# Joint key products, a second key bank, and the spatial gate's statistics, norm and scaling on other engines

## Chip, cores and metric

One core of one Trainium2 chip runs the kernel. The metric is the device time of one execution in microseconds (us), as the median of several runs.

## What is computed

The kernel is a two-layer encoder on 512 positions of width 1024. The change touches the first mixer of each layer, which is two head groups side by side: attention over a low-rank cache (8 heads, keys of 64 + 32 columns), and a spatial gate. Cut to that part:

```python
for l in range(DEPTH):                                   # 2 layers
    h = rmsnorm(x, norm_mix_g[l]); proj = h @ w_in[l]
    # A: attention, 8 heads
    q  = rmsnorm(h_q) @ w_uq;  q_nope, q_pe = split, rope
    kv = rmsnorm(h_kv) @ w_ukv;  k_nope, v = split       # (512, 8, 64) each
    s  = q_nope @ k_nope.T + q_pe @ k_pe.T
    o_mla = softmax(s * scale) @ v
    # B: spatial gate
    u, v = split(gelu(h_sg))                             # 512 columns each
    v = layernorm(v, ln_g, ln_b)
    o_sg = u * (W_s @ v + b)                             # per head, in chunks of 128 positions
    x = x + concat(rmsnorm(o_mla), rmsnorm(o_sg)) @ w_out
    ...                                                  # memory attention, gated MLP
```

## The kernel before

**Numbers in halves.** Every factor of a product is split into a rounded part and a remainder (`_hi`, `_lo`), and each product is three matmuls (`product3`, L1387 to L1389): hi by hi, hi by lo, lo by hi. Weights come in blocks through `raw`; ScalarE rounds a block (`split`, L459), GpSimd takes the remainder (`low`, L358), and TensorE uses both. There are four slots, and `ahead(b)` rounds block b + 3.

**Steps.** Attention runs over 8 heads h and 4 blocks t of 128 queries. A step is the pair (h, t), with i = 4h + t. Each engine has its own program with this loop written out by hand, and tables such as `STAT_STEPS` say in which step an extra piece stands. Engines wait for each other only by counting semaphores (`need`), and each engine keeps strictly to its own order. In step i:

- TensorE: `scores(i+4)` (three matmuls into one of banks 5, 6, 7, once `exps(i+1)` is done), `turn(i)` (four transposes of the exponentials into bank i % 2, L1543, once `exps(i)` and `turned_lo(i-2)` are done); at t = 0 `spread_sums(h-1)` (L1571); at t = 1 and 2 half of `attend(h-1)` each; at t = 3 `q_proj(h+3)`, and at t = 1 `k_proj(h+2)`.
- ScalarE: `exps(i+3)` (L606, with a sum over the row), `turned_hi(i)` (L614), and at fixed steps `q_part` (L593), `k_part` (L600), `copy_sums` (L622), a block to round (L459) and pieces of the gate.
- VectorE: `amax(i+4)` (L1085), `turned_lo(i)` (L1111), and at fixed steps `q_part` (L1062), `k_part` (L1067), `attended` (L1097), `recip_sums` and pieces of the gate.
- GpSimd: `low` for the blocks, and the remainders of queries (`query_low`, L371) and of the gate's normed input (`gate_low`, L376).

**Banks of the keys.** Each head's key product fills 64 of 128 rows, and from head 2 on it shares bank 4 with the query product:

```python
def q_bank(h):
    return (4, 6)[h] if h < 2 else 4

def k_bank(h):
    return (5, 7)[h] if h < 2 else 4
```

So `k_proj(h)` waits until VectorE has read the query (`qf_done`), and `q_proj(h+1)` until VectorE has read the key (`kl_done`).

**The gate.** ScalarE's GELU writes `vt` (L655). VectorE takes its mean and variance (`statistics`, L1115 and L1117), ScalarE and VectorE make the inverse root (`small_root`), VectorE normalises (L1170, L1172, two operations a chunk), ScalarE rounds (L695), GpSimd takes the remainder. TensorE mixes in four parts (`mix`, bank 2), VectorE gates `u` (L1127), ScalarE squares it (L684) and later scales it (L688), and TensorE turns it (`turn_gated`, L1600) in head 7.

## Time and profile before

| | us |
|---|---|
| median of 3 runs (lowest, highest) | 1498.18 (1496.62, 1498.19) |
| profiled execution: its time | 1497.97 |
| profiled execution: its span | 1496.2 |
| TensorE busy | 1460.7 |
| VectorE busy | 748.4 |
| ScalarE busy | 692.1 |
| GpSimd busy | 646.5 |

Matmuls overlap in the array, so TensorE's busy time counts the overlap as well, and it is not the number of matmuls times their pitch. What a stage loses is seen from the starts of its matmuls and from the idle time that the timeline prints before a row, with the instruction that ended it.

### The profile page before, as it was taken

What the parts mean: (1) busy time and instruction counts of PE and PEld (TensorE: products, weight loads), DVE (VectorE), ACT (ScalarE), POOL (GpSimd) and SP (SyncE); (2) the same over time, 40 slices, a digit from 0 to 9 for tenths busy, and PEclk for the clock granted to TensorE, in tenths of its full rate; (3) what the DMA queues carried; (4) which work ended last, traced back from release to release, by engine and by line L of the source; (5) the groups of instructions that cost most, each with busy time, mean ns of one, the idle gap of its engine ahead of it and who ended that gap; (6) DMA issues with size and microseconds to landing.
All of it is one profiled execution on the core that took longest, in us unless ns stands there. A gap on an engine that the chain in (4) does not pass through costs nothing.

```text
span 1496.2 us, 19445 instructions
## 1 busy us (share of the span) xinstructions
PE 1460.7 (98%) x6876; PEld 1196.7 (80%) x6876; DVE 748.4 (50%) x1154; ACT 692.1 (46%) x1107; POOL 646.5 (43%) x313
## 2 busy tenths in 40 slices
PE   8999999999999999999999999999999999999996
PEld 7776689888888888888878776888888888888884
DVE  7648578343355420445264776781526544024534
ACT  6566746354354421344355775553534444124432
POOL 2433148644343554354445322684343454435350
PEclk9999999999999999999999999999999999999998
DMA  5320225412233333232323102453031332323231
GB/s 204 101 82 15 70 82 158 143 56 71 61 106 101 112 99 99 85 104 80 121 80 98 55 29 71 127 183 99 29 99 57 113 112 81 116 85 100 77 91 57
DMA packets 38888, 138.75 MB, mean 93 GB/s; under 512 B 4448, under 2 KB 4704, under 8 KB 38560
## 3 DMA queue, kind: packets, MB, share of 16 engines
q1 hardware_dynamic: 37872, 134.25, 29.3%
q10 hardware_dynamic: 944, 3.51, 0.7%
q8 instruction: 49, 0.80, 0.2%
q14 instruction: 23, 0.19, 0.0%
HBM read 135.64 MB, written 2.10 MB: 92 GB/s over the span
## 4 chain that ended last, share of the span: by engine, by line
PE 74%; issue 10%; DVE 8%; ACT 4%; POOL 4%; DMA 0%; SPq 0%; POOLq 0%; DVEq 0%; ACTq 0%
PE ps L1387 24%; PE ps L1388 24%; PE ps L1389 24%; POOL w_lo L358 4%; DVE small L1085 1%; ACT work L606 1%; DVE h_lo L1111 1%; DVE arena L1111 1%; DVE work L1170 0%; PE ps L1543 0%; DMA raw<-blocks_d 0%; DVE arena L1067 0%; ACT arena L614 0%; DVE work L1062 0%; DVE work L1097 0%
## 5 line engine op out<-in xcount | busy, mean ns | idle before, releaser
L358 POOL TENSOR_TENSOR w_lo<-raw,w_hi 128x1024 fp32r<-128x1024 f32 x244 | 594.5, 2454 | 704.4 <-ACT w_hi L459 704.4
L1387 PE MATMUL ps<-h_hi,w_hi 128*128 128x512 f32 (+1 forms) x1040 | 406.0, 390 | 3.5 <-DVE w_lo L900 1.7
L459 ACT ACTIVATE w_hi<-raw 128x1024 fp32r<-128x1024 f32 x247 | 255.0, 1054 | 330.8 <-PE ps L1389 327.8
L1389 PE MATMUL ps<-h_hi,w_lo 128*128 128x512 f32 (+1 forms) x1040 | 403.1, 388 | 0.0
L1388 PE MATMUL ps<-h_lo,w_hi 128*128 128x512 f32 (+1 forms) x1040 | 403.1, 388 | 0.0
L1387 PE MATMUL ps<-arena,w_hi 128*128 128x512 f32 (+2 forms) x656 | 244.3, 372 | 4.4 <-DVE work L1062 2.4
L1389 PE MATMUL ps<-arena,w_lo 128*128 128x512 f32 (+2 forms) x656 | 241.9, 369 | 0.0
L1388 PE MATMUL ps<-arena,w_hi 128*128 128x512 f32 (+2 forms) x656 | 241.8, 369 | 0.0
L1387 PEld LDWEIGHTS ps<-h_hi,w_hi 128*128 128x128 f32 x1040 | 195.2, 188 | 47.3 <-issue 3.1
L1388 PEld LDWEIGHTS ps<-h_lo,w_hi 128*128 128x128 f32 x1040 | 195.3, 188 | 40.6 <-issue 1.0
L1389 PEld LDWEIGHTS ps<-h_hi,w_lo 128*128 128x128 f32 x1040 | 195.2, 188 | 40.1
L1286 DVE TENSOR_TENSOR work<-ps,work 128x512 f32<-128x512 f32 x88 | 54.7, 684 | 216.6 <-PE ps L1389 215.7
L1387 PEld LDWEIGHTS ps<-arena,w_hi 128*128 128x128 f32 (+1 forms) x656 | 122.8, 187 | 29.3 <-DVE work L1062 5.4
L1200 DVE TENSOR_TENSOR x<-x,ps 128x512 f32<-128x512 f32 x60 | 37.5, 683 | 205.7 <-PE ps L1389 205.7
L1389 PEld LDWEIGHTS ps<-arena,w_lo 128*128 128x128 f32 (+1 forms) x656 | 122.8, 187 | 21.8
L1388 PEld LDWEIGHTS ps<-arena,w_hi 128*128 128x128 f32 (+1 forms) x656 | 122.9, 187 | 20.0
L815 ACT ACTIVATE work<-work,par 128x512 f32<-128x512 f32 x88 | 64.8, 806 | 111.2 <-DVE work L1286 111.2
L1297 DVE SCALAR_TENSOR_TENSOR work<-work,par 128x511 f32<-128x511 f32 x88 | 66.1, 752 | 12.0 <-DVE work L1294 3.1
L1294 DVE SCALAR_TENSOR_TENSOR work<-work,par 128x511 f32<-128x511 f32 x88 | 68.6, 780 | 0.0
L1085 DVE TENSOR_REDUCE small<-ps 128x1 f32<-128x512 f32 x64 | 43.5, 680 | 35.9 <-PE ps L1389 35.4
L1387 PE MATMUL ps<-arena 128*128 128x512 f32 (+2 forms) x160 | 59.9, 374 | 0.0
L821 ACT ACTIVATE work<-work 128x512 f32<-128x512 f32 x44 | 27.9, 633 | 60.5 <-DVE work L1297 60.3
(185 smaller groups left out, 1780.7 us busy)
## 6 DMA issues: line engine op xcount, KB each, us to landing
raw<-blocks_d SPq DMA_DIRECT2D x247, 512.0 KB, 3.5
work<-memT_d ACTq DMA_DIRECT2D x2, 1024.0 KB, 4.9
outT_d<-work SPq DMA_DIRECT2D x8, 256.0 KB, 2.2
x<-xT_d SPq DMA_DIRECT2D x3, 512.0 KB, 7.5
work<-ln_d ACTq DMA_DIRECT2D x2, 512.0 KB, 3.6
x<-xT_d SPq DMA_DIRECT2D x2, 256.0 KB, 4.5
raw<-blocks_d SPq DMA_DIRECT2D x2, 256.0 KB, 4.9
par<-par_d ACTq DMA_DIRECT2D x2, 113.5 KB, 3.9
```

The source lines that it names most:

```text
L358: gp.tensor_tensor(w_lo[:, b % SPLIT, :], raw[:, b % RAW, :], w_hi[:, b % SPLIT, :].bitcast(F32), ALU.subtract).then_inc(lo_done.sem, 1)
L459: act.activation(w_hi[:, b % SPLIT, :], raw[:, r, :], ACT.Copy).then_inc(hi_done.sem, 1)
L815: act.activation(conv[:, bank + 2 * j + s, :], lin[:, 2 * j + s, :], ACT.Identity, bias=cb, scale=cw).then_inc(tap1.sem, 1)
L1085: dve.tensor_reduce(low_score[:, i % 4:i % 4 + 1], ps[BS[i % 3]][:, :], AXX, ALU.min)\
L1111: dve.tensor_tensor(pt_lo[h % 2][:, :, c], ps[i % 2][:, :].rearrange("p (k q) -> p k q", k=TT), pt_hi[h % 2][:, :, c].bitcast(F32), ALU.su ...
L1200: dve.tensor_tensor(x[:, t0 + j, :], x[:, t0 + j, :], ps[banks[j]][:, :], ALU.add)\
L1286: dve.tensor_tensor(lin[:, 2 * j + s, :], ps[bank + 2 * s + j][:, :], rs, ALU.mult)\
L1294: dve.scalar_tensor_tensor(out=c[:, 1:SEQ], in0=a[:, 0:SEQ - 1], scalar=col(C_W0 + at), in1=c[:, 1:SEQ], op0=ALU.mult, op1=ALU.add).then_i ...
L1297: dve.scalar_tensor_tensor(out=c[:, 0:SEQ - 1], in0=a[:, 1:SEQ], scalar=col(C_W2 + at), in1=c[:, 0:SEQ - 1], op0=ALU.mult, op1=ALU.add).th ...
L1387: pe.matmul(out, a_hi, b_hi, start=first, stop=False)
L1388: pe.matmul(out, a_hi, b_lo, start=False, stop=False)
L1389: return pe.matmul(out, a_lo, b_hi, start=False, stop=last)
```

## The change

1. **Keys.** The keys of heads 2p and 2p + 1 come from one product of 128 rows (`k_proj(p)`): four in a layer, not eight, at steps (0, 1), (2, 1) and (4, 1) after the first. It goes to bank 5 for the first pair and to bank 2 after it, apart from the query in bank 4. The even head's half is split as before. The odd head's half sits in rows 64 to 127, so ScalarE copies it to `k_odd`, rounds it from there (`k_second`), and GpSimd takes its remainder (`key_low`).
2. **Statistics.** The GELU of `vt` also sums its rows. VectorE makes the mean in step (0, 0), and ScalarE squares the four chunks around it, with a sum, in steps (0, 1), (0, 2), (0, 2), (0, 3).
3. **Norm.** VectorE subtracts and scales in one operation a chunk, in steps (1, 0) to (1, 3); GpSimd multiplies by the gain and adds the offset, two operations a chunk (`gate_norm`). ScalarE rounds the result in (2, 0) to (2, 3).
4. **Later gating.** The third and fourth `mix` move to (4, 3) and (5, 1), the last one into bank 4. Squares and root follow later, and the scaling of `u` moves from ScalarE to VectorE, in steps (6, 2) and (6, 3).
5. `copy_sums` stands ahead of `turned_hi` in its step, the spread of the sums fills 64 rows, and two weight blocks change places.

```diff
-STAT_STEPS = ((0, 1), (0, 2), (0, 3), (1, 0))
-ROOT_STEP = (1, 1)
-NORM_STEPS = ((1, 2), (1, 3), (2, 2), (2, 3))
-SPLIT_STEPS = ((1, 3), (2, 0), (2, 3), (3, 0))
+STAT_STEPS = ((0, 1), (0, 2), (0, 2), (0, 3))
+ROOT_STEP = (1, 0)
+NORM_STEPS = ((1, 0), (1, 1), (1, 2), (1, 3))
+SPLIT_STEPS = ((2, 0), (2, 1), (2, 2), (2, 3))
-MIX_STEPS = ((3, 2), (3, 3), (4, 2), (4, 3))
+MIX_STEPS = ((3, 2), (3, 3), (4, 3), (5, 1))
...
-        def k_bank(h):
-            return (5, 7)[h] if h < 2 else 4
+        def k_bank(p):
+            return 5 if p == 0 else 2
...
+                def key_low(p):
+                    need(kh_done, 2 * p + 2)
+                    gp.tensor_tensor(k_lo[0:64, 1, :], k_odd[:, :], k_hi[0:64, 1, :].bitcast(F32), ALU.subtract)\
+                        .then_inc(kodd_done.sem, 1)
+                def gate_norm(t):
+                    need(vs_done, t + 1)
+                    gp.tensor_tensor(vt[:, t, :], vt[:, t, :], ln_gb[:, 0, :], ALU.mult).then_inc(vg_mul.sem, 1)
+                    need(vg_mul, t + 1)
+                    gp.tensor_tensor(vt[:, t, :], vt[:, t, :], ln_gb[:, 1, :], ALU.add).then_inc(vn_done.sem, 1)
...
+                def k_even(p):
+                    block_used(B_HEAD[p])
+                    act.activation(k_hi[0:64, 0, :], ps[k_bank(p)][0:64, :], ACT.Copy).then_inc(kh_done.sem, 1)
+                    if p > 0:
+                        need(kodd_done, p)
+                    act.activation(k_odd[:, :], ps[k_bank(p)][64:128, :], ACT.Copy).then_inc(kst_done.sem, 1)
+                def k_second(p):
+                    need(kst_done, p + 1)
+                    act.activation(k_hi[0:64, 1, :], k_odd[:, :], ACT.Copy).then_inc(kh_done.sem, 1)
...
+                    for c in range(TT):
+                        if (h, t) == STAT_STEPS[c]:
+                            need(vmean, 1)
+                            act.activation(sv_hi[:, c, :], vt[:, c, :], ACT.Square, bias=nmean[:, c:c + 1],
+                                           accum_out=vsq[:, c:c + 1]).then_inc(vsq_done.sem, 1)
...
-                    for c in SCALED_STEPS.get((h, t), ()):
-                        need(gated_root, 1)
-                        act.activation(u[:, c, :], u[:, c, :], ACT.Copy, scale=sm_t[:, c:c + 1])\
-                            .then_inc(sg_normed.sem, 1)
...
+                        dve.tensor_scalar(vt[:, g, :], vt[:, g, :], nmean[:, g:g + 1], sm_t[:, g:g + 1], ALU.add, ALU.mult)\
+                            .then_inc(vs_done.sem, 1)
...
+                    for c in SCALED_STEPS.get((h, t), ()):
+                        dve.tensor_scalar(u[:, c, :], u[:, c, :], sm_t[:, c:c + 1], None, ALU.mult).then_inc(sg_normed.sem, 1)
...
                     if h >= 2:
-                        need(kl_done, h)
+                        need(qf_done, h)
...
+                    c = slice(4 * P, 4 * P + 2 * NOPE)
+                    if p > 1:
+                        need(rsum_done, 2 * p - 2)
...
+                    product3(ps[k_bank(p)][:, :], wh[:, 0, c], wl[:, 0, c], ckv_hi[:, 0, :], ckv_lo[:, 0, :],
+                             True, True).then_inc(used.sem, 1)
```

TensorE, step (1, 1), before: one turn, half of `attend(0)` (the 64x512 products from `arena`), then `k_proj(3)` with its wait for the query, then the next scores.

```order
L1543 MATMUL ps<-ident,work 128x128 [waits ptl_done,exp_done]
L1543 MATMUL ps<-ident,work 128x128 x3
L1387 MATMUL ps<-arena 64x512 [waits ptl_done]
L1388 MATMUL ps<-arena 64x512
L1389 MATMUL ps<-arena 64x512
L1387 MATMUL ps<-arena 64x512
L1388 MATMUL ps<-arena 64x512
L1389 MATMUL ps<-arena 64x512
L1387 MATMUL ps<-arena,w_hi 64x512 [waits qf_done]
L1388 MATMUL ps<-arena,w_hi 64x512
L1389 MATMUL ps<-arena,w_lo 64x512
L1387 MATMUL ps<-arena 128x512 [waits exp_done]
```

The same step after the change:

```order
L1579 MATMUL ps<-ident,work 128x128 [waits ptl_done,exp_done]
L1579 MATMUL ps<-ident,work 128x128 x3
L1421 MATMUL ps<-arena 64x512 [waits ptl_done]
L1422 MATMUL ps<-arena 64x512
L1423 MATMUL ps<-arena 64x512
L1421 MATMUL ps<-arena 64x512
L1422 MATMUL ps<-arena 64x512
L1423 MATMUL ps<-arena 64x512
L1421 MATMUL ps<-arena 128x512 [waits exp_done]
L1422 MATMUL ps<-arena 128x512
```

The three key products and their wait are gone from this step; this also holds for steps (3, 1) and (5, 1).

ScalarE, from head 0's first `turned_hi` (to `arena`, waits `turned`) on, before. The rows on `work,small` are exponentials:

```order
L614 ACTIVATE arena<-ps 128x4x128 [waits turned]
L459 ACTIVATE w_hi<-raw 128x1024 [waits used,raw_in1]
L593 ACTIVATE arena<-work 128x512 [waits qf_done]
L606 ACTIVATE work,small<-ps,small 128x512 [waits turned,nmax_done]
L614 ACTIVATE arena<-ps 128x4x128 [waits turned]
L600 ACTIVATE arena<-ps 64x512 [waits kp_mm]
L606 ACTIVATE work,small<-ps,small 128x512 [waits turned,nmax_done]
L614 ACTIVATE arena<-ps 128x4x128 [waits turned]
L606 ACTIVATE work,small<-ps,small 128x512 [waits turned,nmax_done]
L614 ACTIVATE arena<-ps 128x4x128 [waits turned]
```

The same stretch after the change, from the second exponential on; L721 is the square with a sum, L632 the copy to `k_odd`:

```order
L642 ACTIVATE work,small<-ps,small 128x512 [waits turned,nmax_done]
L650 ACTIVATE arena<-ps 128x4x128 [waits turned]
L629 ACTIVATE arena<-ps 64x512 [waits used]
L632 ACTIVATE k_odd<-ps 64x512 [waits kodd_done]
L721 ACTIVATE h_hi,small<-work,small 128x512 [waits vmean]
L642 ACTIVATE work,small<-ps,small 128x512 [waits turned,nmax_done]
L650 ACTIVATE arena<-ps 128x4x128 [waits turned]
L721 ACTIVATE h_hi,small<-work,small 128x512 [waits vmean] x2
L642 ACTIVATE work,small<-ps,small 128x512 [waits turned,nmax_done]
L650 ACTIVATE arena<-ps 128x4x128 [waits turned]
L721 ACTIVATE h_hi,small<-work,small 128x512 [waits vmean]
```

Four squares and one more copy now stand among head 0's exponentials.

GpSimd in heads 0 to 2, before (L371 is `query_low`, L376 `gate_low`, L358 `low`):

```order
L371 TENSOR_TENSOR arena<-work,arena 128x512 [waits qh_done]
L358 TENSOR_TENSOR w_lo<-raw,w_hi 128x1024 [waits hi_done]
L371 TENSOR_TENSOR arena<-work,arena 128x512 [waits qh_done]
L376 TENSOR_TENSOR h_lo<-work,h_hi 128x512 [waits svh_done]
L371 TENSOR_TENSOR arena<-work,arena 128x512 [waits qh_done]
L376 TENSOR_TENSOR h_lo<-work,h_hi 128x512 [waits svh_done] x3
```

And after (L379 `query_low`, L384 `key_low`, L389 and L391 `gate_norm`, L395 `gate_low`, L366 `low`):

```order
L379 TENSOR_TENSOR arena<-work,arena 128x512 [waits qh_done]
L366 TENSOR_TENSOR w_lo<-raw,w_hi 128x1024 [waits hi_done]
L379 TENSOR_TENSOR arena<-work,arena 128x512 [waits qh_done]
L384 TENSOR_TENSOR arena<-k_odd,arena 64x512 [waits kh_done]
L389 TENSOR_TENSOR work<-work 128x512 [waits vs_done,ln_in]
L391 TENSOR_TENSOR work<-work 128x512 [waits vg_mul]
L389 TENSOR_TENSOR work<-work 128x512 [waits vs_done]
L391 TENSOR_TENSOR work<-work 128x512 [waits vg_mul]
L379 TENSOR_TENSOR arena<-work,arena 128x512 [waits qh_done]
L389 TENSOR_TENSOR work<-work 128x512 [waits vs_done]
L391 TENSOR_TENSOR work<-work 128x512 [waits vg_mul]
L395 TENSOR_TENSOR h_lo<-work,h_hi 128x512 [waits svh_done]
```

Eight operations of the norm now stand between queries and gate remainders, and the third chunk's stands behind head 4's query.

## Rows read from the trace of the kernel before

Times are in us; "L" numbers are lines of the kernel before. The two layers run the same code.

**Rows 1.** The page, its first part: busy time of each engine over the span.

```profile
PE 1460.7 (98%) x6876; PEld 1196.7 (80%) x6876; DVE 748.4 (50%) x1154; ACT 692.1 (46%) x1107; POOL 646.5 (43%) x313
```

**Rows 2.** Windows: interval, length, busy PE, PEld, DVE, ACT, POOL (instructions), granted clock.

```profile
94.71:104.05 9.34, 8.40 (x45) 6.48 (x44) 6.98 (x14) 7.59 (x16) 3.62 (x2) 1.00 0.16 51
104.05:114.14 10.09, 10.03 (x54) 7.42 (x53) 9.56 (x21) 6.73 (x17) 1.29 (x1) 1.00 0.08 33
114.14:125.82 11.68, 10.21 (x54) 7.34 (x53) 10.17 (x17) 8.36 (x18) 3.81 (x3) 1.00 0.01 1
...
158.88:167.26 8.38, 7.25 (x42) 5.25 (x41) 6.55 (x16) 7.63 (x19) 0.00 (x0) 1.00 0.00 0
...
94.71:175.92 81.21, 74.64 (x416) 56.01 (x415) 64.91 (x122) 62.52 (x141) 24.65 (x15) 1.00 0.10 31
828.20:909.33 81.13, 74.60 (x416) 55.98 (x415) 64.89 (x122) 62.51 (x140) 24.66 (x15) 1.00 0.10 31
```

**Rows 3.** Timeline, TensorE, heads 0 to 3 of layer 0: start, length, ..., idle before.

```profile
101.87 0.50 PE L1387 MATMUL ps<-arena,w_hi 128*128 128x512 f32 x1 [0.94 <-DVE arena L1067]
...
103.36 0.39 PE L1387 MATMUL ps<-arena 128*128 128x512 f32 x1
103.59 0.39 PE L1388 MATMUL ps<-arena 128*128 128x512 f32 x1
...
116.67 0.63 PE L1543 MATMUL ps<-ident,work 128*128 128x128 f32 x4 [0.80 <-DVE h_lo L1111]
...
119.35 0.45 PE L1387 MATMUL ps<-arena,w_hi 128*64 128x512 f32 x1 [0.67 <-DVE work L1062]
...
128.20 0.63 PE L1543 MATMUL ps<-ident,work 128*128 128x128 f32 x4 [0.65 <-DVE arena L1111]
...
130.75 0.45 PE L1387 MATMUL ps<-arena,w_hi 128*64 128x512 f32 x1 [0.53 <-DVE work L1062]
```

**Rows 4.** Timeline: ScalarE's GELUs of `u`, and the first product after head 0's keys.

```profile
66.93 2.42 ACT L586 ACTIVATE work<-ps,small 128x512 f32<-128x512 f32 x4
...
69.41 0.50 PE L1387 MATMUL ps<-w_hi,h_hi 128*128 128x512 f32 x1
```

**Rows 5.** Timeline, ScalarE in head 2: a copy, an exponential, a copy.

```profile
122.00 0.59 ACT L600 ACTIVATE arena<-ps 64x512 fp32r<-64x512 f32 x1
122.48 0.68 ACT L606 ACTIVATE work<-ps,small 128x512 f32<-128x512 f32 x1
...
123.15 0.59 ACT L614 ACTIVATE arena<-ps 128x512 fp32r<-128x512 f32 x1
```

**Rows 6.** Timelines, and one line's summary: scalings on VectorE, and GpSimd's operations.

```profile
43.00 0.43 DVE L1034 TENSOR_SCALAR work<-work 128x512 f32<-128x512 f32 x1
...
108.35 1.29 POOL L371 TENSOR_TENSOR arena<-work,arena 128x512 fp32r<-128x512 f32 x1 [6.37 <-ACT arena L593]
...
L1179 DVE TENSOR_SCALAR small<-small x2: 151/152/153, 160.2 to 893.6; 128x4 f32<-128x4 f32 x2
...
268.31 2.33 DVE L1226 TENSOR_SCALAR small<-small 128x4 f32<-128x4 f32 x1
...
263.49 9.47 POOL L358 TENSOR_TENSOR w_lo<-raw,w_hi 128x1024 fp32r<-128x1024 f32 x4
```

**Rows 7.** Timeline, TensorE at the start of head 7.

```profile
167.26 0.63 PE L1543 MATMUL ps<-ident,work 128*128 128x128 f32 x4 [1.13 <-DVE arena L1111]
...
168.62 0.66 PE L1600 MATMUL ps<-ident,work 128*128 128x128 f32 x4 [0.29 <-ACT work L688]
...
170.58 0.63 PE L1543 MATMUL ps<-ident,work 128*128 128x128 f32 x4 [1.31 <-DVE arena L1111]
```

**Rows 8.** Timeline, ScalarE in the last two steps of head 6.

```profile
163.92 1.33 ACT L688 ACTIVATE work<-work,small 128x512 f32<-128x512 f32 x2
165.15 0.68 ACT L606 ACTIVATE work<-ps,small 128x512 f32<-128x512 f32 x1
...
167.23 1.33 ACT L688 ACTIVATE work<-work,small 128x512 f32<-128x512 f32 x2
```

173 lines of the change are left out of this document (93 added, 80 removed).

## The prediction

> **What bounds the kernel now.** I read the page first: TensorE is busy for 98% of the span, the other engines for half of it or less [rows 1]. So a saving elsewhere counts only where TensorE waits for it. The windows then show the stage that the change touches, from the first turn of head 0 to the first output product. It lasts 81.2 us in layer 0 and 81.1 in layer 1, with the same busy times within 0.1, so I work out one layer and double it. The granted clock is 1.00 (2.4 GHz) all through, and no term is taken for it [rows 2]. Last, the timeline gives the price of a product: matmuls that follow each other start 0.23 apart although each is shown as 0.39 long [rows 3]. Where TensorE waits, it loses the printed idle time and also the 0.16 (0.39 less 0.23) of overlap.
>
> In heads 0 to 3 TensorE waits five times, each time for VectorE [rows 3]. Three times it is a shared bank: q_proj waits for the key to be read (0.94), k_proj for the query (0.67 and 0.53). Twice it is `turned_lo` that comes late (0.80 and 0.65). VectorE is busy for 9.56 of the 10.09 us of head 1 and 10.17 of 11.68 in head 2 [rows 2]: it is the second bound there. At the start of head 7 TensorE waits three times more: 1.13, 0.29, 1.31 [rows 7]. In those steps ScalarE does its two pairs of scalings of `u`, 1.33 each, and an exponential starts only behind the first pair [rows 8].
>
> **What the change can give, for one layer.**
> 1. Key products. Twelve matmuls go. The three at the start save nothing: the V projection after them needs the last GELU of `u`, which ends at 69.35 (66.93 + 2.42), and starts at 69.41 in any case [rows 4]. Nine are left: 9 x 0.23 = 2.1 us.
> 2. Bank waits. 0.94 + 0.67 + 0.53 and 3 x 0.16 make 2.6. After the change q_proj waits only for the query before it, and k_proj(p) for `copy_sums`, a step or more old or ahead of `turned_hi`. A shorter one of some 0.2 in head 1 prints no idle time. I take 2.8.
> 3. Late `turned_lo`. 0.80 + 0.65 + 2 x 0.16 = 1.8. VectorE loses the statistics, a key half every second head, and one of two norm operations.
> 4. Head 7. 1.13 + 0.29 + 1.31 + 3 x 0.16 = 3.2.
>
> Together 9.9 us a layer: the ceiling.
>
> **What it takes back, for one layer.** I follow the engines from the first turn, with slots (start to start) from the rows: a copy on ScalarE 0.48, an exponential with its sum 0.67 [rows 5]; a remainder or a maximum on VectorE about 0.6 (most of head 1's 21 instructions are of these kinds, and they fill 9.56 us with the two long norm operations at its end).
>
> *Heads 0 and 1.* ScalarE gets the four GELU sums (each the difference 0.67 - 0.48 = 0.19; only the last delays it), four squares with a sum and the second key copy. A square is at least a copy and at most an exponential with a sum, 0.48 to 0.67; I take 0.61, nearer to the latter since it has the sum too. That is 2.4 + 0.5 + 0.2 = 3.1 us more in a head of 9.34 in which it was busy for 7.59 [rows 2]. It becomes the limit of head 0. By my reckoning turns 4 to 6 still come about 1 us sooner, because VectorE no longer holds back the maxima. Then, in step (1, 0), VectorE must wait for ScalarE's root, and its small operations and scalings meet GpSimd.
>
> *The meeting of VectorE and GpSimd.* A scaling of 128x512 in SBUF takes 0.43 alone, and one of only 128x4 takes 0.15 [rows 6]. But one of 128x4 took 2.33 us at 268.31, while GpSimd ran its block remainders without a break (9.47 / 4 = 2.37 each). It waited for GpSimd's operation to end. The change puts four scalings in steps (1, 0) to (1, 3), next to GpSimd's key remainder and `gate_norm` at 1.29 each. Each scaling costs 0.43 alone and up to 1.72 behind one operation; I take 0.9 on average, half an operation of waiting. Then `turned_lo(7)` ends near 115.2 where it was 116.5, and head 2 begins about 0.8 earlier than before, not the 2.1 that the gone stalls and product would give. **Taken back: 1.3**, and 0.3 more until turn 10.
>
> The Trainium skill, page "SBUF — State Buffer", section "Who interferes with whom", says that a VectorE scaling in the two-port mode and a GpSimd operation exclude each other, and the one issued second blocks for the whole instruction. The trace agrees with the 2.33 us above. Without such an exclusion the sum below would be about 1 us a layer better; with it the sum stays.
>
> *Heads 2 and 3.* GpSimd's chain sets when ScalarE may round the normed chunks. Chunk 2 stands behind `query_low(4)`, which needs head 4's query. Turn 8 near 113.3 (0.8 before 114.14) starts that step, the maximum, query and remainder on VectorE follow `turned_lo(7)` of 115.2 and a scaling of up to 1.3, so the query is there near 117.7 and rounded near 118.3. Then come 1.29 (query), 2.6 (norm 2), 1.3 (remainder 0), 2.6 (norm 3): chunk 3 is ready near 126.1. ScalarE reaches that rounding in step (2, 3) near 123.9 and stands still for 2.2 us, behind a wait of 1.7 for chunk 2, and the exponentials of the next step stand behind it. TensorE has about two steps of slack, because `turn(i)` needs only `turned_lo(i-2)`. I take 0.8 us for what comes through at turn 14. Remainder 3 is done near 130, and TensorE reaches `mix(0)` just after. **Taken back: 0.8.**
>
> *Heads 4 and 5.* The moved mixes carry the same matmuls; waits for `gated` stay. About 0.4 at most is lost; I take it as 0 to 0.4, and 0.
>
> *Head 7.* The scalings of `u` leave ScalarE, so turn 28 no longer waits. But VectorE does them in (6, 2) and (6, 3), two each time, and `turn_gated(0)` needs all four. Two cost 0.9 alone; the second pair meets the remainder of a block that GpSimd starts after step (6, 2), up to 2.37. I take TensorE's wait there as 1.9, from a last scaling at about 168.7 against a TensorE that is ready at 166.9. **Taken back: 1.9.**
>
> **The sum.** 9.9 - 1.3 - 0.3 - 0.8 - 1.9 = 5.6; two layers give 11.2. From the profiled execution's 1497.97 that makes 1486.8, and the median lies 0.2 above that execution: 1487. Nothing after the stage should change but its start. As landmarks in layer 0: the turn at 114.14 comes 0.8 earlier, the one at 125.82 2.3, that at 158.88 4.4, the first output product (175.92) 5.6.
>
> **Rivals.**
> - *Most of the ceiling arrives* (chance 0.12). If scalings and GpSimd seldom meet and ScalarE's waits stay in the slack, only a part of 0.8 in heads 0 and 1 is lost: 9.1 a layer, 1480 (1478 to 1482). For it: GpSimd is busy for 1.29 us in all of head 1 and 3.81 in head 2 [rows 2]. Against it: the 10.3 us of `gate_norm` go just there.
> - *GpSimd's chain pushes back* (0.17). Each VectorE operation that shuts it out, and each block that comes between, makes ScalarE's wait longer, and beyond the slack every us of it is a us of TensorE. With 2 to 4 us more a layer the gain is 2 to 3.7 a layer: 1490 to 1495.
> - *Within 0.2%* (0.09): 0.2%, 3.0 us, is about what a measurement of this kernel can tell from no change. It needs some 4.5 to 7 us a layer of such pushing back, or a head 0 that is longer by ScalarE's whole 3.1 us together with the 1.9 of head 7 doubled: about 1497.
> - *Slower* (0.07). `mix(0)` in step (3, 2) waits for the last gate remainder, and ScalarE for chunk 3. The eight operations of 1.29, four remainders of 1.29 and two or three others make some 19 us of GpSimd in one row. If they are slowed by half through VectorE's exclusion, the last remainder comes at 139, not 130, TensorE stands for 8 us a layer, and the time is 1498 + 2 x (8 - 5.6) = 1503. It decides from 5.6 us on.
> - *The forecast itself* (0.55): 1482 to 1490.
>
> So faster has 0.84, the same 0.09, slower 0.07. The range for 8 in 10 takes the forecast's own band, most of the first rival and most of the second: 1479 to 1494.
>
> **What would show it.** The key products: 24 matmuls fewer on L1387's successors; no wait of k_proj or q_proj of more than 0.3. Head 0: squares between exponentials, exponential waits for VectorE gone, ScalarE near full. The exclusion: some of the eight scalings of 128x512 in a layer longer than 0.6, and a spread from 0.43 to beyond 1.3. The chain: ScalarE idle before the third and fourth rounding of the gate's input, about 2 us each. Head 7: one wait of TensorE before the first turn of gated `u`, ended by a scaling on VectorE, and none before turn 28. What would make it wrong: TensorE waiting for exponentials in head 0 by more than 1 us, or before `mix(0)`.

## The result, and the profile after

The changed kernel takes 1510.71 us (median of 4 runs, 1510.17 to 1512.46) against 1497.40 of the kernel before beside it: a ratio of 1.0091, interval 1.0074 to 1.0109. It is 13 us slower, where 11 us faster was forecast. The profiled execution took 1512.46 us.

The page of after, first part, answers to [rows 1]. TensorE has 24 matmuls fewer, as the change says, and yet 2.8 us more of busy time:

```profile
PE 1463.5 (97%) x6852; PEld 1201.0 (80%) x6852; DVE 745.0 (49%) x1132; ACT 699.5 (46%) x1131; POOL 678.0 (45%) x337
```

Windows of after, with the columns of [rows 2]: head 0, head 1, head 2, head 7, the whole stage in either layer, and two pieces inside heads 2 and 7.

```profile
95.41:104.19 8.78, 8.44 (x45) 6.38 (x43) 5.57 (x12) 8.72 (x19) 3.64 (x2) 1.00 0.12 37
104.19:114.69 10.50, 9.80 (x51) 6.97 (x52) 8.68 (x17) 9.18 (x24) 4.67 (x4) 1.00 0.13 47
114.69:130.11 15.42, 11.85 (x55) 8.71 (x54) 11.01 (x17) 10.61 (x23) 12.97 (x11) 0.89 0.01 2
169.09:183.09 14.00, 9.49 (x48) 7.34 (x49) 9.60 (x14) 7.34 (x15) 4.75 (x2) 0.63 0.24 75
95.41:183.09 87.68, 76.59 (x407) 58.25 (x406) 63.20 (x112) 65.33 (x147) 38.89 (x26) 0.92 0.11 34
835.43:923.50 88.07, 76.86 (x408) 58.50 (x406) 63.32 (x112) 65.59 (x148) 38.93 (x26) 0.92 0.11 34
122.00:126.00 4.00, 4.00 (x13) 3.12 (x14) 2.04 (x3) 2.80 (x6) 3.92 (x4) 0.57 0.00 0
174.70:181.00 6.30, 6.24 (x25) 4.83 (x26) 2.15 (x5) 3.01 (x7) 2.36 (x1) 0.57 0.30 85
```

The stage takes 87.7 and 88.1 us where it took 81.2 and 81.1 [rows 2]: 6.5 and 6.9 us more, 13.4 together. That is nearly all of the result. By head (the turn of a head's step 0 to that of the next), with the trace of before read at the same turns:

| head | before | after | change | forecast |
|---|---|---|---|---|
| 0 and 1 | 19.43 | 19.28 | -0.15 | -0.8 |
| 2 | 11.68 | 15.42 | +3.74 | -1.5 |
| 3 | 12.86 | 10.59 | -2.27 | with heads 4 and 5: -2.1 |
| 4 and 5 | 20.20 | 19.21 | -0.99 | |
| 6 and 7 | 17.04 | 23.18 | +6.14 | -1.2 |

Two places hold the loss. The timeline of TensorE after shows both, and what follows them:

```profile
122.00 0.69 PE L1421 MATMUL ps<-arena,w_hi 128*128 128x512 f32 x1 [2.40 <-ACT work L658]
...
122.92 0.63 PE L1423 MATMUL ps<-arena,w_lo 128*128 128x512 f32 x1
123.34 0.63 PE L1421 MATMUL ps<-arena 128*128 128x512 f32 x1
...
169.09 0.63 PE L1579 MATMUL ps<-ident,work 128*128 128x128 f32 x4 [1.96 <-DVE arena L1153]
...
174.76 1.11 PE L1644 MATMUL ps<-ident,work 128*128 128x128 f32 x4 [4.51 <-DVE work L1215]
...
177.81 0.63 PE L1421 MATMUL ps<-arena 128*64 128x512 f32 x1
178.23 0.63 PE L1422 MATMUL ps<-arena 128*64 128x512 f32 x1
```

At 122.00 it is the key product of pair 2 in step (2, 1). It waits 2.40 us for `copy_sums` (L658), because the product now goes to bank 2 and the sums of head 1 are still in it. At 174.76 it is the first turn of the gated `u`, which waits 4.51 us for a scaling on VectorE (L1215); turn 28 ahead of it waits 1.96 for `turned_lo`. And behind either long wait matmuls start 0.42 or 0.43 apart, not 0.23 [rows 3]: the granted clock is 0.57 over 122.0 to 126.0 and over 174.7 to 181.0, a mixture of TensorE's lower level (1.2 GHz, which the windows show as 0.50) and its upper one. Layer 1 shows the same waits, 2.39, 2.01 and 4.61, and 0.60 and 0.51 in stretches of the same length behind the first and the last. Of the old waits of heads 0 to 3 [rows 3], those at bank 4 and the one before turn 13 are gone; the one of 0.80 before turn 9 has grown to 1.17, and four small ones of 0.17 to 0.34 are new in head 1.

In head 7 the level was down before the long wait. Windows of after, inside the 5.7 us between turn 28 and the gated turn:

```profile
169.60:170.30 0.70, 0.65 (x6) 0.28 (x3) 0.70 (x1) 0.69 (x3) 0.70 (x1) 0.73 0.04 12
170.30:172.00 1.70, 0.00 (x0) 0.00 (x0) 1.70 (x2) 0.00 (x0) 1.30 (x1) 0.50 0.00 0
```

The clock reached 0.50 about 1 us behind turn 28, which had waited 1.96, and stayed there through the 4.51 us in which TensorE had nothing to do.

**Who is late at the key product.** ScalarE, after, at the end of step (2, 0) and in step (2, 1):

```profile
119.65 0.63 ACT L625 ACTIVATE arena<-work 128x512 fp32r<-128x512 f32 x1 [2.10 <-DVE work L1104]
120.19 0.61 ACT L737 ACTIVATE h_hi<-work 128x512 fp32r<-128x512 f32 x1
120.71 0.67 ACT L642 ACTIVATE work<-ps,small 128x512 f32<-128x512 f32 x1
...
121.37 0.58 ACT L658 ACTIVATE work<-ps 64x512 f32<-64x512 f32 x1
```

`copy_sums` stands behind the query's rounding (L625), a rounding of the gate's input (L737) and an exponential (L642), and the query's rounding waits 2.10 us for VectorE. VectorE, after, just before that:

```profile
114.08 1.57 DVE L1205 TENSOR_SCALAR work<-work,small 128x512 f32<-128x512 f32 x1
115.58 0.68 DVE L1127 TENSOR_REDUCE small<-ps 128x1 f32<-128x512 f32 x1
...
116.78 0.67 DVE L1153 TENSOR_TENSOR h_lo<-ps,h_hi 128x512 fp32r<-128x512 f32 x1
117.38 1.05 DVE L1205 TENSOR_SCALAR work<-work,small 128x512 f32<-128x512 f32 x1
118.34 0.68 DVE L1127 TENSOR_REDUCE small<-ps 128x1 f32<-128x512 f32 x1
118.94 0.67 DVE L1104 TENSOR_TENSOR work<-ps,turn_q 128x512 f32<-128x512 f32 x1
```

It works without a gap. The last two norm scalings (L1205) take 1.57 and 1.05 us where one alone takes 0.43 [rows 6], beside `gate_norm` on GpSimd, and the query (L1104) stands behind both.

**Who is late in head 7.** VectorE, after, in steps (6, 1) to (7, 0):

```profile
165.18 0.69 DVE L1153 TENSOR_TENSOR arena<-ps,arena 128x512 fp32r<-128x512 f32 x1 [0.95 <-ACT arena L650]
165.79 0.68 DVE L1147 TENSOR_TENSOR work<-work 128x512 f32<-128x512 f32 x1
166.39 0.17 DVE L1212 TENSOR_SCALAR small<-small 128x4 f32<-128x4 f32 x1
167.06 0.16 DVE L1027 TENSOR_TENSOR small<-small 128x4 f32<-128x4 f32 x1 [0.51 <-ACT small L549]
...
167.66 0.69 DVE L1127 TENSOR_REDUCE small<-ps 128x1 f32<-128x512 f32 x1
168.26 0.68 DVE L1153 TENSOR_TENSOR arena<-ps,arena 128x512 fp32r<-128x512 f32 x1
...
168.94 2.94 DVE L1215 TENSOR_SCALAR work<-work,small 128x512 f32<-128x512 f32 x2
171.81 0.68 DVE L1127 TENSOR_REDUCE small<-ps 128x1 f32<-128x512 f32 x1
172.51 0.68 DVE L1139 TENSOR_TENSOR work<-ps,work 64x512 f32<-64x512 f32 x1
173.23 0.69 DVE L1153 TENSOR_TENSOR arena<-ps,arena 128x512 fp32r<-128x512 f32 x1
173.84 0.87 DVE L1215 TENSOR_SCALAR work<-work,small 128x512 f32<-128x512 f32 x2
```

Between one `turned_lo` (165.18) and the next (168.26) stand the addition of the squares (L1147) and the whole gate root, 1.3 us with its wait for ScalarE. That makes turn 28 late. Then the first pair of scalings takes 2.94 us. The summary of the line says how that splits (shortest, median and longest, in ns):

```profile
L1215 DVE TENSOR_SCALAR work<-work,small x8: 456/478/2573, 168.9 to 914.2; 128x512 f32<-128x512 f32 x8
```

GpSimd's timeline says why:

```profile
169.21 2.39 POOL L366 TENSOR_TENSOR w_lo<-raw,w_hi 128x1024 fp32r<-128x1024 f32 x1 [9.74 <-ACT w_hi L491]
```

Most of these scalings take 0.46 to 0.48 us, and the longest 2.57: the pair ends at 171.88, 0.3 us behind GpSimd's block remainder of 2.39 us (171.60). The maximum, the attended values and a `turned_lo` queue behind it on VectorE, and only then comes the pair for which TensorE waits.

The Trainium skill, page "SBUF — State Buffer", section "Who interferes with whom", describes such an exclusion between a VectorE scaling in the two-port mode and a GpSimd operation. By that rule, the trace agrees: 0.46 alone, 2.57 beside an operation of 2.39.

### The profile page after: what moved, and what is told of

Its sections match the earlier page's. It is cut to its first block, busy times and chain, and to the rows that moved or that the text cites. A ratio compares the mean times of both kernels' runs of the same rounds, so it can differ in the third digit from the quotient of the medians.

```text
span 1510.6 us, 19421 instructions
## 1 busy us (share of the span) xinstructions
PE 1463.5 (97%) x6852; PEld 1201.0 (80%) x6852; DVE 745.0 (49%) x1132; ACT 699.5 (46%) x1131; POOL 678.0 (45%) x337
## 4 chain that ended last, share of the span: by engine, by line
PE 77%; issue 9%; DVE 6%; POOL 4%; ACT 4%; DMA 0%; SPq 0%; POOLq 0%; DVEq 0%; ACTq 0%
PE ps L1421 25%; PE ps L1422 25%; PE ps L1423 25%; POOL w_lo L366 4%; PE ps L1579 1%; DVE small L1127 1%; ACT work L642 1%; DVE work L1215 0%; DVE work L1205 0%; DMA raw<-blocks_d 0%; ACT arena L650 0%; PE ps L1644 0%; DVE h_lo L1153 0%; DVE arena L1284 0%; DVE work L1399 0%
## 5 line engine op out<-in xcount | busy, mean ns | idle before, releaser
L366 POOL TENSOR_TENSOR w_lo<-raw,w_hi 128x1024 fp32r<-128x1024 f32 x244 | 595.0, 2456 | 698.7 <-ACT w_hi L491 698.7
L1421 PE MATMUL ps<-arena,w_hi 128*128 128x512 f32 (+1 forms) x648 | 241.3, 372 | 4.8 <-ACT work L658 4.8
L1423 PE MATMUL ps<-arena,w_lo 128*128 128x512 f32 (+1 forms) x648 | 239.0, 369 | 0.0
L1422 PE MATMUL ps<-arena,w_hi 128*128 128x512 f32 (+1 forms) x648 | 238.9, 369 | 0.0
L1421 PEld LDWEIGHTS ps<-arena,w_hi 128*128 128x128 f32 x648 | 122.2, 189 | 27.3 <-ACT work L658 6.3
L1423 PEld LDWEIGHTS ps<-arena,w_lo 128*128 128x128 f32 x648 | 122.3, 189 | 20.6
L1422 PEld LDWEIGHTS ps<-arena,w_hi 128*128 128x128 f32 x648 | 122.4, 189 | 19.3
L1421 PE MATMUL ps<-arena 128*128 128x512 f32 (+2 forms) x160 | 61.8, 386 | 0.4 <-ACT work L642 0.4
L1423 PE MATMUL ps<-arena 128*128 128x512 f32 (+2 forms) x160 | 57.2, 358 | 0.0
```

The source lines that it names most:

```text
L366: gp.tensor_tensor(w_lo[:, b % SPLIT, :], raw[:, b % RAW, :], w_hi[:, b % SPLIT, :].bitcast(F32), ALU.subtract).then_inc(lo_done.sem, 1)
L1421: pe.matmul(out, a_hi, b_hi, start=first, stop=False)
L1422: pe.matmul(out, a_hi, b_lo, start=False, stop=False)
L1423: return pe.matmul(out, a_lo, b_hi, start=False, stop=last)
```

## The experiments

My theory after reading the two traces had three parts for each layer: (A) the key product stuck behind `copy_sums`, (B) the gate's last pieces too late in head 7, partly through the exclusion and partly through their place, and (C) the lower clock behind both. The rivals were that VectorE's scaling on its own is the loss, that the moved statistics and norm are, that the key pairs are, or that the clock adds nothing.

The table has after and all twelve runs. "before" is the kernel before, measured beside them; its median moved by 0.8 us at most, so I compare the medians with after's too. "Stage" is the sum of both layers in the profiled run, from the first turn to the first output product, against 162.4 of before; what the whole time differs by beyond it lies mostly ahead of the first turn, which came between 92.9 and 95.4 us in these traces. In a stage whose key product waits 2.4 us, turn 9 to turn 12 takes 12.4 to 12.5 us where the clock falls behind it and 10.9 where it doesn't, as mixes_back shows below. So 1.6 us a layer of a "stage" can come from that alone.

| kernel | us | before | ratio (interval) | stage, change |
|---|---|---|---|---|
| after | 1510.71 | 1497.40 | 1.0091 (1.0074, 1.0109) | +13.4 |
| scale_act | 1504.91 | 1497.07 | 1.0054 (1.0037, 1.0070) | +7.5 |
| block_late | 1505.65 | 1497.07 | 1.0058 (1.0042, 1.0075) | +5.9 |
| sums_first | 1504.81 | 1497.07 | 1.0050 (1.0033, 1.0067) | +7.8 |
| gate_back | 1507.88 | 1497.07 | 1.0073 (1.0057, 1.0090) | +10.9 |
| mixes_back | 1498.61 | 1497.80 | 1.0011 (1.0001, 1.0021) | -0.9 |
| keys_only | 1500.62 | 1497.80 | 1.0029 (1.0018, 1.0040) | +3.6 |
| key_late | 1506.64 | 1497.80 | 1.0061 (1.0044, 1.0078) | +8.5 |
| combo | 1497.71 | 1497.80 | 0.9996 (0.9986, 1.0006) | +0.4 |
| warm_wait | 1504.12 | 1497.87 | 1.0042 (1.0027, 1.0058) | +8.6 |
| root_early | 1503.33 | 1497.87 | 1.0042 (1.0027, 1.0057) | +5.6 |
| best1 | 1493.37 | 1497.87 | 0.9978 (0.9969, 0.9987) | -4.6 |
| best2 | 1492.27 | 1497.87 | 0.9966 (0.9954, 0.9978) | -4.9 |

**scale_act**: the scaling of `u` goes back to ScalarE, in the changed kernel's steps (6, 2) and (6, 3).

```diff
-                    for c in SCALED_STEPS.get((h, t), ()):
-                        dve.tensor_scalar(u[:, c, :], u[:, c, :], sm_t[:, c:c + 1], None, ALU.mult).then_inc(sg_normed.sem, 1)
+                        dve.sem_inc(gated_root.sem, 1)
...
+                    for c in SCALED_STEPS.get((h, t), ()):
+                        need(gated_root, 1)
+                        act.activation(u[:, c, :], u[:, c, :], ACT.Copy, scale=sm_t[:, c:c + 1])\
+                            .then_inc(sg_normed.sem, 1)
```

> The changed kernel, with the scaling of u back on ScalarE, in the same steps (6, 2) and (6, 3) as now. Theory A (the scaling's meeting with GpSimd's block remainder on VectorE is what head 7 loses): the wait of 4.5 us before the turn of gated u falls below 1 us, the clock stays at its upper level there, and 4 to 6 us a layer come back: 1499 to 1503. Rival B (the root and scaling simply come too late, a step or more behind before, whichever engine does them): the wait stays above 3 us and the time above 1507.

Measured: 5.8 us less than after. TensorE's timeline:

```profile
170.25 1.12 PE L1648 MATMUL ps<-ident,work 128*128 128x128 f32 x4 [2.32 <-ACT work L735]
```

The wait of 4.51 is half as long, and it is now ScalarE's scaling that is late. So the engine of the scaling is only a part of the loss in head 7; its step is the rest. Neither theory's number came, and the clock didn't stay at its upper level, as theory A had it: it is 0.66 over the 6 us behind this turn, and 0.50 already behind turn 28, which waits 2.08.

**block_late**: two weight blocks are rounded later, so that no block remainder meets a scaling of `u`.

```diff
-                    if t == 2 and h in (2, 4, 6):
+                    if t == 2 and h in (2, 4):
                         ahead(B_V + 4 + h // 2)
-                    if (h, t) == (7, 0):
+                    if (h, t) == (7, 1):
+                        ahead(B_V + 7)
+                    if (h, t) == (7, 2):
                         ahead(B_OUT)
```

> The changed kernel, with two weight blocks rounded later: the one of step (6, 2) in (7, 1), the one of (7, 0) in (7, 2), so that GpSimd has no block while VectorE scales u. The scaling stays on VectorE. Theory A: the four scalings take 0.43 to 0.6 us each instead of 2.9 for the first pair, the wait before the turn of gated u falls from 4.5 to below 1.5, and the time is 1500 to 1504. Rival B (lateness of the root, or VectorE's own load): scalings shorten but the wait stays above 3 us, time above 1507.

Measured: 5.1 us less than after. The summary of the scaling's line:

```profile
L1217 DVE TENSOR_SCALAR work<-work,small x8: 456/479/482, 165.4 to 905.7; 128x512 f32<-128x512 f32 x8
```

TensorE's timeline:

```profile
169.09 1.12 PE L1646 MATMUL ps<-ident,work 128*128 128x128 f32 x4 [2.28 <-DVE work L1217]
```

With the same scalings on the same engine, none is longer than 0.482 us once the remainder is elsewhere, and the wait falls from 4.51 to 2.28. So the meeting costs 2.2 us of wait in this place, and the same 2.3 us of lateness as in scale_act stays. The expected wait below 1.5 and time below 1504 didn't come. The stage is 3.1 us shorter in layer 1; in layer 0 it is 4.3, because there the clock didn't fall behind the key product.

**sums_first**: `copy_sums` stands ahead of the exponential in its step.

```diff
-                    if i + 3 < HEADS * TT:
-                        exps(i + 3)
                     if t == 1 and h >= 1:
                         copy_sums(h - 1)
+                    if i + 3 < HEADS * TT:
+                        exps(i + 3)
                     turned_hi(i)
```

> The changed kernel, with ScalarE's copy of the sums ahead of the exponential of its step, not behind it. Theory A (the joint key product of step (2, 1) waits for this copy because it shares bank 2 with the sums, and the copy stands behind an exponential that VectorE holds up): the 2.4 us wait before the product in head 2 goes or falls below 1, the stretch at the lower clock behind it goes too, and 2.5 to 4 us a layer come back: 1503 to 1506. Rival C (VectorE is late in heads 1 and 2 through the norm, and whatever waits there only moves): the next turn waits instead and less than 1 us a layer comes back, above 1508.

Measured: 5.9 us less than after. TensorE's timeline at the product:

```profile
120.97 0.50 PE L1421 MATMUL ps<-arena,w_hi 128*128 128x512 f32 x1 [1.72 <-ACT work L658]
```

The window behind it:

```profile
120.97:124.97 4.00, 4.00 (x19) 3.00 (x20) 1.88 (x3) 3.95 (x10) 3.92 (x4) 1.00 0.00 0
```

The wait is 0.68 shorter, not below 1, and turn 9 to turn 12 takes 10.29 us, not 12.52; the time is in the expected range. The other 1.5 us are the clock: 1.00 here over 4 us, 0.57 in after over as many, and (1 - 0.57) x 4.0 = 1.7.

**gate_back**: scale_act with the statistics and the whole norm on VectorE as before; keys and late mixes stay.

```diff
-STAT_STEPS = ((0, 1), (0, 2), (0, 2), (0, 3))
-ROOT_STEP = (1, 0)
-NORM_STEPS = ((1, 0), (1, 1), (1, 2), (1, 3))
-SPLIT_STEPS = ((2, 0), (2, 1), (2, 2), (2, 3))
+STAT_STEPS = ((0, 1), (0, 2), (0, 3), (1, 0))
+ROOT_STEP = (1, 1)
+NORM_STEPS = ((1, 2), (1, 3), (2, 2), (2, 3))
+SPLIT_STEPS = ((1, 3), (2, 0), (2, 3), (3, 0))
...
-                gate_norm(0)
-                gate_norm(1)
                 query_low(4)
-                gate_norm(2)
```

> The keys, the second key bank and the later mixes of the changed kernel, with statistics, norm and the scaling of u as before the change (statistics and norm on VectorE in their old steps, scaling on ScalarE). What differs from the scale_act kernel is statistics and norm alone. Theory A: those cost head 1 and 2 about what the waits in the changed kernel show (1.2 us before turn 9, part of the 2.4 before the key product), so this one is 1 to 3 us a layer faster than scale_act: 1494 to 1499. Rival D (moving them off VectorE is a gain, and only the scaling and the bank were faults): this one is slower than scale_act by 1 us a layer or more, since the old waits of 0.80 and 0.65 come back.

Measured: 3.0 us more than scale_act. The key product's wait is longer, not shorter: 2.98 for `copy_sums`. So moving the statistics and the norm isn't what makes the product wait. Theory A fell and rival D's sign was right, though the old wait of 0.65 isn't back and the one before turn 9 is 1.38. The gain from the move is about 1.5 us a layer by the medians, but the two intervals overlap, and the stages differ by 0.6 us in layer 0 and 2.8 in layer 1, where the clock behind the product is lower (0.50, not 0.60).

**mixes_back**: mixes, squares, root and scaling in their old steps, on the old engines and banks; keys, statistics and norm as changed.

```diff
-MIX_STEPS = ((3, 2), (3, 3), (4, 3), (5, 1))
+MIX_STEPS = ((3, 2), (3, 3), (4, 2), (4, 3))
-GATED_STEPS = ((5, 2), (5, 3), (5, 3), (6, 0))
-GATED_ROOT = (6, 1)
-SCALED_STEPS = {(6, 2): (0, 1), (6, 3): (2, 3)}
+GATED_STEPS = ((5, 0), (5, 1), (5, 1), (5, 2))
+GATED_ROOT = (5, 3)
+SCALED_STEPS = {(6, 1): (0, 1), (6, 2): (2, 3)}
```

> The changed kernel with the whole gating tail as before the change: mixes in (4, 2) and (4, 3) and bank 2, squares, root and scaling of u a half head earlier, scaling on ScalarE. Keys, statistics and norm stay changed. Against scale_act it moves only the steps. Theory A now has two parts in head 7: the scaling's meeting with GpSimd, and the root in step (6, 1), where VectorE also adds a square and then waits for ScalarE, which holds up turn 28 by 2 us and makes the scaling late. If so, the waits of 2.1 before turn 28 and 2.3 before the gated turn shrink to the old 1.1 and 0.3, and 3 to 4 us a layer come back: 1497 to 1500. Rival: the tail's waits come from what is new before it (the backlog of ScalarE in heads 5 and 6), and they stay: 1503 to 1506.

Measured: 12 us less than after, in the expected range, and 0.11% above before (interval 0.01 to 0.21%). Its waits in head 7 are 1.13, 0.29 and 1.31, to the hundredth those of [rows 7]. So most of the net loss hangs on part 4 of the change. The wait of 2.40 at the key product is still there, but in this profiled run no lower clock follows it in either layer: turn 9 to turn 12 takes 10.94 us, not 12.52, so 3.1 us of the stage's gain aren't part 4's. The same happened in other traces. Of the sixteen layers in which the product waits 2.4 to 3.0 us, the clock fell behind it in eleven and stayed at 1.00 in five: both of mixes_back, layer 0 of block_late and of root_early, and layer 1 of keys_only. The ten runs of mixes_back spread from 1496.38 to 1501.78, which may be this; it wasn't followed up.

**keys_only**: mixes_back with the statistics and norm of before, so only the key pairs and what belongs to them are left.

```diff
-STAT_STEPS = ((0, 1), (0, 2), (0, 2), (0, 3))
+STAT_STEPS = ((0, 1), (0, 2), (0, 3), (1, 0))
...
-MIX_STEPS = ((3, 2), (3, 3), (4, 3), (5, 1))
+MIX_STEPS = ((3, 2), (3, 3), (4, 2), (4, 3))
```

> The joint keys and the second bank alone; statistics, norm, mixes, squares, root and scaling all as before the change. Theory A: the key product saves nine matmuls and the bank waits, and loses by its wait for the copy of the sums (3.0 in gate_back, with a stretch at the lower clock) and by the mixes' sharing of bank 2: 1497 to 1502. Rival: the keys are the good part of the change, and the loss was all in the gate: 1487 to 1493.

Measured: 2.8 us slower than before, as theory A had it. The product's wait is 2.98. The pairs save nine matmuls in a layer, 2.1 us by [rows 3], and the old waits at bank 4, and lose more than that. Most of it is lost from turn 9 to turn 12, which takes 13.10 us in layer 0, where the clock falls behind the product, and 11.52 in layer 1, where it doesn't; before took 9.15. Turn 9's wait is 1.39 where it was 0.80. Against mixes_back it is 2.0 us slower: the same sign as gate_back for the statistics and norm.

**key_late**: the key products of steps (2, 1) and (4, 1), those of pairs 2 and 3, and their readers move one step back, behind `copy_sums`; pair 1's stays in (0, 1). TensorE's part:

```diff
-                    if t == 1 and h % 2 == 0 and h + 2 < HEADS:
+                    if t == (1 if h == 0 else 2) and h % 2 == 0 and h + 2 < HEADS:
```

> The changed kernel with the joint key product of pairs 1 and 2 (after the first) one step later, at t = 2, and its readers with it. The copy of the sums then has a whole step before the product needs bank 2. Theory A: the wait of 2.4 us in head 2 goes, the lower clock behind it too, and 3 to 4 us a layer come back: 1502 to 1505. Rival C (VectorE is late in heads 1 and 2, so a wait of the same size comes at the next turn): less than 1 us a layer, above 1508.

Measured: 4.1 us less than after, where 5.7 to 8.7 were expected. The wait in head 2 is gone, and turn 9 to turn 12 takes 8.76 us, not 12.52. A new wait of 0.79 comes up before the spread of the sums in (5, 0), for VectorE's gating, and head 7 keeps its waits of 2.01 and 4.30. So part A costs 3.8 us a layer where it stands, with its clock. Head 3 gives 0.9 of it back (11.52 us, not 10.59), as it does in best1 (11.54), and head 5 another 0.8, with the new wait, which best1 doesn't have. Pair 3's product had no wait in after, so its shift bought nothing.

**combo**: key_late, sums_first and block_late together, with the gate's last pieces one step earlier, the scaling still on VectorE.

```diff
-GATED_STEPS = ((5, 2), (5, 3), (5, 3), (6, 0))
-GATED_ROOT = (6, 1)
-SCALED_STEPS = {(6, 2): (0, 1), (6, 3): (2, 3)}
+GATED_STEPS = ((5, 2), (5, 2), (5, 3), (5, 3))
+GATED_ROOT = (6, 0)
+SCALED_STEPS = {(6, 1): (0, 1), (6, 2): (2, 3)}
```

> All remedies together on the changed kernel: key product at t = 2, copy of the sums first, squares in (5, 2) and (5, 3), root in (6, 0), scaling on VectorE in (6, 1) and (6, 2), the block of (6, 2) in (7, 1) and that of (7, 0) in (7, 2). Theory A: both new waits gone, what stays are the 2.1 us of products and the old waits saved less some 2 us in heads 0 and 1: 1488 to 1494, faster than before. Rival: a further wait takes their place (ScalarE in head 5 with four squares in two steps, or the output product waiting for its blocks): 1496 to 1500.

Measured: 13 us less than after, and no difference from before: the rival's range. Turn 28 still waits 1.95 and the turn after it 0.96, the wait of 0.79 in (5, 0) is there as in key_late, and the clock is at 0.50 behind turn 28 in both layers.

**warm_wait**: the changed kernel, with 16 matmuls whose result is not used in TensorE's wait before the first gated turn.

```diff
+                        need(gated, SG_HEADS)
+                        for _ in range(16):
+                            pe.matmul(ps[4][:, :], k_hi[:, 0, 0:P], k_hi[:, 0, :], start=True, stop=True)
                         need(sg_normed, 4)
```

> The changed kernel with 16 extra matmuls of 512 columns, whose result nothing uses, in TensorE's wait before the first turn of gated u (some 3.7 us of work in a wait of 4.5). The wait itself stays as long. If the lower clock behind it is the consequence of TensorE's idleness in the wait, the pitch of the matmuls after it is 0.23 and not 0.43, and 2 to 3 us a layer come back: 1505 to 1507. Rival: the pitch there is held by something else (VectorE, ScalarE, the array's operands): the time stays at 1510 to 1512.

Measured: 6.6 us less than after. TensorE's timeline, with the added matmuls at 167.77:

```profile
167.77 5.51 PE L1640 MATMUL ps<-arena 128*128 128x512 f32 x16
173.13 0.60 PE L1647 MATMUL ps<-ident,work 128*128 128x128 f32 x4
...
174.69 0.39 PE L1421 MATMUL ps<-arena 128*64 128x512 f32 x1
174.91 0.39 PE L1422 MATMUL ps<-arena 128*64 128x512 f32 x1
```

Windows of warm_wait, in the first of these matmuls and in the last:

```profile
167.77:169.80 2.03, 2.03 (x8) 1.65 (x6) 2.03 (x2) 0.38 (x1) 1.72 (x1) 0.53 0.02 4
171.80:173.10 1.30, 1.30 (x7) 1.01 (x6) 1.30 (x4) 0.82 (x1) 0.40 (x1) 1.00 0.57 230
```

So they start at the lower level, which fell behind turn 28 as in after, and the level comes back while they run: they take 5.5 us, not the expected 3.7. The first gated turn comes 6.2 us after turn 28 (173.13 less 166.95), in after 5.7 (174.76 less 169.09). But the products that follow are 0.22 apart, not 0.42. The stage is 2.1 us shorter in layer 0 and 2.6 in layer 1, 4.7 of the 6.9 between the two profiled runs. The rest of it lies ahead of the first turn (93.28 against 95.41), in instructions that are the same in both kernels: after's first 20 us had a granted clock of 0.91, warm_wait's 1.00. So only 4.7 us are shown to belong to the experiment, and they come from the clock: no wait was shortened.

**root_early**: the changed kernel with all three of combo's tables for squares, root and scaling, and nothing else. The root's:

```diff
-GATED_ROOT = (6, 1)
+GATED_ROOT = (6, 0)
```

> The changed kernel with squares in (5, 2) and (5, 3), root in (6, 0) and the scaling in (6, 1) and (6, 2), still on VectorE, blocks where they are. Theory: the root in (6, 1) shares its step with a square's addition on VectorE, and the two waits between VectorE and ScalarE delay turn 28 by some 2 us; one step earlier, the wait before turn 28 falls from 2.0 to below 1, and the scalings of (6, 1) no longer meet the block that GpSimd takes after (6, 2): the 4.5 us wait falls to about 1: 1500 to 1504. Rival: the second pair, in (6, 2), still runs with the block, and the waits only change places: above 1506.

Measured: 7.4 us less than after, in the expected range, but not as expected. The gated turn's own wait of 4.51 is gone in layer 0 and 0.60 in layer 1, but turn 28 still waits 1.96, and the turn behind it 1.01. The clock is down to 0.50 behind turn 28 here too, without a wait of 4.5 us after it. I had put turn 28 down to the root standing in one step with the addition of the squares, and that fell. VectorE's timeline shows what stands there in its place:

```profile
162.00 0.69 DVE L1153 TENSOR_TENSOR arena<-ps,arena 128x512 fp32r<-128x512 f32 x1 [0.35 <-ACT arena L650]
162.61 0.68 DVE L1147 TENSOR_TENSOR work<-work 128x512 f32<-128x512 f32 x1
163.21 0.88 DVE L1215 TENSOR_SCALAR work<-work,small 128x512 f32<-128x512 f32 x2
164.00 0.68 DVE L1127 TENSOR_REDUCE small<-ps 128x1 f32<-128x512 f32 x1
164.60 0.68 DVE L1153 TENSOR_TENSOR arena<-ps,arena 128x512 fp32r<-128x512 f32 x1
```

The addition and a pair of scalings, 1.4 us, now fill the gap between two `turned_lo` that the root filled in after, and the root stands one step ahead. best2, below, has the same five rows and the root two steps ahead, and its turn 28 waits 0.97. So the root's place is worth about 1 us there; this is read from traces, and no run changed it alone: mixes and squares differ as well.

**best1**: mixes_back with sums_first, and pair 2's key product alone one step later.

```diff
-                    if t == 1 and h % 2 == 0 and h + 2 < HEADS:
+                    if t == (2 if h == 2 else 1) and h % 2 == 0 and h + 2 < HEADS:
```

> Joint keys, new statistics and norm; the copy of the sums first in its step; the key product of pair 2 alone one step later; gating tail and scaling as before the change. Against mixes_back only the wait of head 2 is mended. If that wait is all that keeps this kernel from its products: 2 to 3 us a layer under mixes_back, 1492 to 1495, faster than before. Rival: VectorE's lateness in heads 1 and 2 takes it back: 1496 to 1499.

Measured: 1493.37, faster than before by 0.22%. Its stage is 1.8 us a layer shorter than that of mixes_back, which had part A's wait without a lower clock: 1.3 of it lies between turns 9 and 16, and 0.4 before turn 28, which waits 0.69 and not 1.13.

**best2**: best1, but the scaling on VectorE in the old steps (6, 1) and (6, 2), and the blocks of block_late.

```diff
+                    if (h, t) == (7, 1):
+                        ahead(B_V + 7)
+                    if (h, t) == (7, 2):
                         ahead(B_OUT)
```

> As best1, but with the scaling of u on VectorE in the old steps (6, 1) and (6, 2), and with the two weight blocks of (6, 2) and (7, 0) in (7, 1) and (7, 2), so that nothing of GpSimd meets it. The old waits of head 7 (1.13, 0.29, 1.31) should go: 2 to 3 us a layer under best1, 1487 to 1491. Rival: the later blocks hold up the output product, or the later scaling's own 0.9 us a pair holds up the turns: equal to best1 or slower.

Measured: 1492.27, faster than before by 0.34%, and the fastest seen; but 1487 to 1491 was expected, and its interval overlaps that of best1, so the scaling's move to VectorE is not shown to gain anything. Window of the stage in layer 0:

```profile
93.21:171.90 78.69, 73.25 (x408) 54.91 (x406) 60.44 (x112) 65.01 (x148) 36.65 (x26) 1.00 0.08 25
```

TensorE's waits at the start of head 7:

```profile
163.68 0.63 PE L1580 MATMUL ps<-ident,work 128*128 128x128 f32 x4 [0.97 <-DVE arena L1154]
166.57 0.63 PE L1580 MATMUL ps<-ident,work 128*128 128x128 f32 x4 [1.39 <-DVE arena L1154]
```

Only the old wait of 0.29 is gone; 0.97 and 1.39 stand where 1.13 and 1.31 were. The clock is 1.00, and the stage is 2.5 us a layer shorter than before (78.73 us in layer 1): about 45% of the 5.6 that were forecast for the change as it was made.

## Why the prediction was wrong

The forecast was 5.6 us a layer less, and the stage came out 6.5 more in layer 0: 12.1 apart. The rows account for 11.4 of it: 2.4 for the key product's wait, 1.7 for the clock behind it, 2.0 for turn 28, 2.6 for the gated turn (4.51 where 1.9 was taken), and (1 - 0.57) x 6.3 = 2.7 for the clock behind that. The remaining 0.7 is a balance: turn 9's wait of 1.17, which was to be gone, and 0.65 lost in heads 0 and 1, less 1.2 gained in heads 3 to 5.

**The step that failed first: "Bank waits".** It took `copy_sums` to be "a step or more old or ahead of `turned_hi`" whenever k_proj(p) needs it. For pair 2 both stand in the same step (2, 1). Being ahead of `turned_hi` didn't help: three other operations of ScalarE are ahead of `copy_sums`, and the first of them waits 2.10 us for VectorE. The price is 2.40 us of wait. key_late and best1 take the wait away and get the time back; keys_only has it with nothing else of the change but the pairs, and longer. What the step said of the old waits at bank 4 was right: they are gone.

**The second: "Head 7".** 1.9 us were to be taken back by one wait, and turn 28 was to wait no longer. It waits 1.96, and the gated turn 4.51. The mechanism of the exclusion was right and its price too (the forecast allowed up to 2.37; the scaling lost 2.1), though it was the first pair that met the remainder, not the second. What was missed is the queue on VectorE. The root and the addition of the squares, now in step (6, 1), stand ahead of a maximum and a `turned_lo`; and the second pair of scalings stands behind a maximum, the attended values and a `turned_lo`, which all move back with the first. Of the wait of 4.51, block_late assigns 2.2 to the meeting with GpSimd; the other 2.3 are the late steps, since they stay with the scaling on either engine and are gone in mixes_back and nearly so in root_early (0 and 0.60).

**The third: the clock.** "No term is taken for it", because it was 1.00 through the whole stage of before. That stage had no wait over 1.31 [rows 3, 7]. Behind the wait of 2.40, and behind turn 28's of 1.96, the level fell, for 4.4 us a layer by the windows (1.7 + 2.7). Two direct readings agree roughly. Behind the key product it is 1.6 us, since turn 9 to turn 12 takes 12.5 us with the fall and 10.9 without it, at the same wait. In head 7 warm_wait gave back 2.1 and 2.6 us. So of the 12.1 us a layer between forecast and result, 7.0 are waits, 4.4 the clock, and 0.7 the balance above.

**A smaller one: "Late `turned_lo`".** 1.8 us were to come from the waits before turns 9 and 13. The second is gone, the first is 1.17 where it was 0.80. `turned_lo(7)`, which the forecast put 1.3 us earlier, ended at 117.45, 22.0 us into the stage where before had 21.8: it stands behind the norm scaling of 1.57 us, which ran beside `gate_norm`.

**What held.** The nine matmuls went and the first three saved nothing: the V projection still starts behind the last GELU of `u`, after a wait of 0.74. The norm scalings took 0.55, 0.94, 1.57 and 1.05 us in layer 0, mean 1.03, where 0.9 was taken. Heads 0 and 1 gained little (0.15 for 0.8), and ScalarE is full in head 0, as forecast (8.72 of 8.78 us). Heads 3 to 5 gained 3.3 where 2.1 was forecast: GpSimd's chain kept up, and ScalarE's third and fourth rounding, which were to stand still for 1.7 and 2.2 us, waited for nothing, partly because the late key product had taken the time already. In best2, which doesn't have that wait, the fourth still waits only 0.21, so this term was too large. The rival "slower" was right in its sign and wrong in its place: `mix(0)` doesn't wait. Neither sign that was to show the forecast wrong appeared (the longest wait for an exponential is 0.19); the ones that failed are "no wait of k_proj of more than 0.3" and "none before turn 28".

A slip in the forecast's working changes nothing: in the second rival, 2 to 4 us off 5.6 leave 1.6 to 3.6, not 2 to 3.7.

**What stays open.** How much of the key product's wait comes from the two long norm scalings, and how much from the order on ScalarE, was not separated: with the norm of before the wait is 2.98, so undoing the split doesn't shorten it. Why the level fell behind the key product in eleven layers of sixteen and not in the other five is open too.
